# Starting an S5 and ConvFFN trunk on one core: the first modulation batches loaded ahead of x, low halves of x shared differently, column thirds dealt 4, 3, 3, 3, 3, 1, 0, and the first gating unit begun beside the last turns

## What is computed

```
mods = silu(c) @ w_ada + b_ada
h = x * (1 + scale) + shift
u = h @ s5_w_in                       # 64 groups of 16 channels
states = scan(a_bar, b_bar u)         # complex, 64 states a group
y = gelu(re(c_bar states) + d_skip u)
z = y @ w_glu
out = z[..., :1024] * sigmoid(z[..., 1024:])
x = layer_norm(ALPHA * x + gate * out)
```

## Time and profile before

| | |
|---|---|
| median of 3 runs | 2645.55 us (2645.07 to 2648.68) |
| profiled execution, its own time | 2644.4 us |
| its span in the profile | 2642.6 us |
| TensorE (PE) busy | 2444.6 us, 93% |
| VectorE (DVE) busy | 1441.1 us, 55% |
| GpSimd (POOL) busy | 1131.5 us, 43% |
| mean granted TensorE clock | 0.966 |

### The profile page before, as it was taken

How to read it: one execution, slowest core, us unless ns; L and a number is a source line. 1 busy time by engine, 2 the same in 40 slices (tenths; PEclk the granted TensorE clock), 3 DMA queues, 4 the chain that set the end, 5 groups by cost and what they waited for, 6 DMA issues and landing times.

```text
span 2642.6 us, 37011 instructions
## 1 busy us (share of the span) xinstructions
PE 2444.6 (93%) x15428; PEld 2334.2 (88%) x15428; DVE 1441.1 (55%) x1957; ACT 631.1 (24%) x1275; POOL 1131.5 (43%) x613
## 2 busy tenths in 40 slices
PE   3798899879999999999989999987999999999995
PEld 2688799679999999999968999976999999999993
DVE  6698321474555555555573344367455555555555
ACT  2433211242222222222121110103322222222213
POOL 4787343263443434343336333415544444444420
PEclk7899999989999999999989999988999999999998
DMA  5435533102222222221101221100111111111102
GB/s 215 152 117 139 185 105 110 51 25 72 80 80 74 79 79 73 80 72 57 64 17 53 75 78 48 41 26 15 57 48 48 45 44 48 49 48 45 44 25 72
DMA packets 90669, 187.28 MB, mean 71 GB/s; under 512 B 27664, under 2 KB 49936, under 8 KB 90384
## 3 DMA queue, kind: packets, MB, share of 16 engines
q1 hardware_dynamic: 80976, 175.23, 20.4%
q10 hardware_dynamic: 9536, 9.77, 1.1%
HBM read 170.66 MB, written 14.32 MB: 70 GB/s over the span
## 4 chain that ended last, share of the span: by engine, by line
PE 82%; DVE 8%; DVEq 2%; issue 2%; DMA 2%; ACT 1%; POOL 1%; SPq 1%; POOLq 1%; ACTq 0%
PE bank L669 17%; PE bank L671 17%; PE bank L670 17%; PE bank L912 8%; PE bank L913 7%; PE bank L914 7%; PE bank L931 2%; PE bank L633 1%; DVE X L1726 1%; DVE ROWS L1718 1%; DMA FST<-s_y 1%; DVE HL L1754 1%; DVE X L1712 1%; PE bank L639 1%; PE bank L976 1%
## 5 line engine op out<-in xcount | busy, mean ns | idle before, releaser
L669 PE MATMUL bank<-HH,WH 128*128 128x344 f32 x2880 | 924.5, 321 | 0.0
L670 PE MATMUL bank<-HL,WH 128*128 128x344 f32 x2880 | 919.9, 319 | 0.0
L671 PE MATMUL bank<-HH,WL 128*128 128x344 f32 x2880 | 919.8, 319 | 0.0
L493 POOL TENSOR_TENSOR WH<-RAW,ZERO 128x1024 fp32r<-128x1024 f32 x176 | 373.0, 2119 | 1191.2 <-DMA RAW<-in_wstream 1104.1
L1692 DVE SCALAR_TENSOR_TENSOR X<-bank,MOD,X 128x344 f32<-128x344 f32 (+1 forms) x624 | 355.5, 571 | 428.1 <-PE bank L914 295.6
L669 PEld LDWEIGHTS bank<-HH,WH 128*128 128x128 f32 x2880 | 540.9, 188 | 15.1 <-issue 13.4
L671 PEld LDWEIGHTS bank<-HH,WL 128*128 128x128 f32 x2880 | 541.3, 188 | 0.0
L670 PEld LDWEIGHTS bank<-HL,WH 128*128 128x128 f32 x2880 | 540.9, 188 | 0.0
L488 POOL TENSOR_TENSOR WL<-RAW,WH 128x1024 fp32r<-128x1024 f32 x188 | 504.4, 2683 | 49.0 <-ACT WH L1024 35.2
L912 PE MATMUL bank<-GH,WH 128*128 128x344 f32 x1248 | 409.5, 328 | 22.2 <-DVE X L1692 22.2
L913 PE MATMUL bank<-GL,WH 128*128 128x344 f32 x1248 | 402.4, 322 | 0.0
(11 more groups left out here) (286 smaller groups left out, 2420.9 us busy)
## 6 DMA issues: line engine op xcount, KB each, us to landing
RAW<-in_wstream SPq DMA_DIRECT2D x188, 512.0 KB, 3.6
ADA<-in_wada SPq DMA_DIRECT2D x20, 2048.0 KB, 9.6
FST<-in_wada SPq DMA_DIRECT2D x8, 1024.0 KB, 7.9
X<-in_xT SPq DMA_DIRECT2D x1, 4128.0 KB, 20.7
out_yT<-X SPq DMA_DIRECT2D x3, 1376.0 KB, 5.6
FST<-in_xT SPq DMA_DIRECT2D x8, 512.0 KB, 4.2
UT<-s_u SPq DMA_DIRECT2D x8, 512.0 KB, 6.0
s_y<-YG ACTq DMA_DIRECT2D x8, 512.0 KB, 2.9
```

What stands on the lines that cost most here:

```text
L493: ptt(WH[:, slot, :], RAW[:, slot, :], bc(ZERO[:, :], [128, 1024]), add).then_inc(s_hi, 1)
L669: pe.matmul(o, wh, hh, start=k == 0, stop=False)
L670: pe.matmul(o, wh, hl, start=False, stop=False)
L671: m = pe.matmul(o, wl, hh, start=False, stop=k == KC - 1)
```

## The change

On SP, all batches of w_ada move ahead of the chunks of x that they are not needed for, and b, H0 and x 6 and 7 change places. TensorE forms the products of batch 1 before the first unit. The sample columns of x are split by GpSimd alone. GpSimd keeps the low halves of x 0 and 1, VectorE takes 2 to 7 in between its small work; `sample_starts` moves behind `output_matrix(0)`. The table LO is built in two parts. The 17 thirds behind third 0 are dealt 4, 3, 3, 3, 3, 1, 0. Chunks 0 to 3 of gating unit 0 go into turn 6 and chunks 4 and 5 into turn 7, first for thirds 0 and 1 of the columns alone; the last third follows behind `toeplitz(7)`. In turn 6 GpSimd's `rotations(7)` stands behind `low_y(0)` and `low_y(1)`. The loads of y and of the toeplitz rows change places on SP, and the reload of x is cut into chunks 0 and 1 ahead of `load_y(7)` and the rest behind it. The diff, cut to what matters:

```diff
...
         BK = [ctx.enter_context(nc.psum_tensor(f"bank{i}", [128, 512], F32)) for i in range(8)]
         SMP_IN, SMP_OUT = BK[7][:, 256:320], BK[7][:, 320:352]
-        SMP_Y = BK[6][:, 0:NS * (KC - 2)], BK[7][:, 0:NS * 2]
...
             load_unit(0)
             load_unit(1)
+            load_first(1)
             load_x(0)
-            sp.dma_start(H0[:, :, :, :], h0T).then_inc(s_h0l, 16)
-            load_first(1)
             load_x(1)
             load_first(2)
-            for i in range(2):
-                sp.dma_start(BR[:, i], bT[i]).then_inc(s_cst4, 16)
             load_x(2)
             load_x(3)
             load_first(3)
+            for i in range(2):
+                sp.dma_start(BR[:, i], bT[i]).then_inc(s_cst4, 16)
             load_x(4)
             load_x(5)
+            load_x(6)
+            load_x(7)
             for dst, src in ((CR[:, 0], cS[0]), (CR[:, 1], cS[1]), (DSK[:, :], dT), (E16[:, :], eye16), (PM[:, :, :], pmask)):
                 sp.dma_start(dst, src).then_inc(s_cst2, 16)
-            load_x(6)
-            load_x(7)
+            sp.dma_start(H0[:, :, :, :], h0T).then_inc(s_h0l, 16)
             load_unit(2)
             load_unit(3)
...
-            load_u(2)
-            load_toeplitz(1)
-            for j in range(2, KC - 2):
+            for j in range(1, KC - 2):
+                load_u(j + 1)
                 load_toeplitz(j)
-                load_unit(j + 5)
-                load_u(j + 1)
+                load_unit(j + 6)
                 if j == 3:
                     load_ada4(1)
+            for k in range(3):
+                load_y(k)
+            load_u(KC - 1)
+            load_y(3)
+            load_y(4)
             load_toeplitz(KC - 2)
-            load_unit(KC + 3)
-            load_y(0)
-            load_y(1)
-            load_u(KC - 1)
-            load_y(2)
-            load_y(3)
+            load_ada4(2)
+            load_y(5)
             load_toeplitz(KC - 1)
-            load_y(4)
-            load_y(5)
-            load_ada4(2)
             load_y(6)
...
-            sp.dma_start(X[:, :, :], xT).then_inc(s_xl, 16)
+            sp.dma_start(X[:, 0:2, :], xT[:, 0:2, :]).then_inc(s_xl, 16)
             load_y(KC - 1)
+            sp.dma_start(X[:, 2:KC, :], xT[:, 2:KC, :]).then_inc(s_xl, 16)
...
-                ptt(HS[:, ks, :], HS[:, ks, :], MOD[:, ks, 1:9], add).then_inc(s_hsf, 1)
-            def low_sample_x(b):
-                ks = slice(2 * b, 2 * b + 2)
-                pool.wait_ge(s_hsh, b + 1)
+                ptt(HS[:, ks, :], HS[:, ks, :], MOD[:, ks, 1:9], add)
+                pool.drain()
+                pool.tensor_copy(HH[:, ks, SEQ:NT], HS[:, ks, :])
+                pool.drain()
                 ptt(HL[:, ks, SEQ:NT], HS[:, ks, :], HH[:, ks, SEQ:NT].bitcast(F32), sub).then_inc(s_hs, 1)
...
             low_half(1)
             sample_x(0)
             low_x(0)
-            low_sample_x(0)
             low_x(1)
+            sample_x(1)
             pool.wait_ge(s_pw, 1)
-            table(LO, 16)
-            sample_x(1)
-            low_x(2)
-            low_sample_x(1)
-            low_x(3)
+            table(LO, 1, 8)
+            sample_x(2)
+            table(LO, 8, 16)
+            sample_x(3)
+            low_half(2)
             pool.tensor_copy(HI[:, :, :, 1], LO[:, :, :, 16])
             pool.drain()
-            table(HI, 7)
-            for b in range(2, 4):
-                sample_x(b)
-                low_sample_x(b)
-            low_half(2)
+            table(HI, 1, 7)
             rotations(0)
             low_half(3)
             state_inputs(1)
-            for j in range(1, KC):
+            for j in range(1, KC - 1):
                 rotations(j)
                 low_half(j + 3)
-                if j < KC - 1:
-                    state_inputs(j + 1)
-            for k in range(KC - 1):
+                state_inputs(j + 1)
+            low_y(0)
+            low_y(1)
+            rotations(KC - 1)
+            for k in range(2, 6):
                 low_y(k)
+            low_half(KC + 2)
+            low_y(6)
             low_half(KC + 3)
...
-            def first_batch(b):
+            def first_products(b):
                 pe.wait_ge(s_first[b], 32)
+                if b:
+                    pe.wait_ge(s_fev, b)
                 for i in (0, 2, 4, 6, 1, 3, 5, 7):
...
                 m.then_inc(s_fprod, 1)
+            def first_sums(b):
                 pe.wait_ge(s_fev, b + 1)
...
-                if k < 4:
+                if k < 2:
                     pe.wait_ge(s_xsp, k + 1)
                 else:
-                    pe.wait_ge(s_xsd, k - 3)
+                    pe.wait_ge(s_xsd, k - 1)
...
             pe.wait_ge(s_scp, 1)
             pe.wait_ge(s_cst, 16 * N_CST)
-            first_batch(0)
+            first_products(0)
+            first_sums(0)
+            first_products(1)
+            first_sums(1)
             pe.wait_ge(s_unit, 2)
             first_units(0)
-            first_batch(1)
             first_units(1)
-            first_batch(2)
+            first_products(2)
+            first_sums(2)
             first_units(2)
-            first_batch(3)
+            first_products(3)
+            first_sums(3)
             for k in range(3, KC):
                 first_units(k)
...
-                if k == 0:
-                    pe.wait_ge(s_unit, N_GLU + u + 1)
-                    if u == 0:
+            def gate_chunk(u, k, thirds=(0, 1, 2)):
+                if k == 0 and u == 0:
+                    if 0 in thirds:
+                        pe.wait_ge(s_unit, N_GLU + 1)
                         pe.wait_ge(s_ev, 24)
+                    else:
                         pe.wait_ge(s_kr, KC)
-                    else:
-                        pe.wait_ge(s_g, KC)
-                        pe.wait_ge(s_yg, 2 * KC)
+                if k == 0 and u == 1:
+                    pe.wait_ge(s_unit, N_GLU + 2)
+                    pe.wait_ge(s_g, KC)
+                    pe.wait_ge(s_yg, 2 * KC)
                 if k < KC - 1:
                     pe.wait_ge(s_hl, k + 1)
                 else:
                     pe.wait_ge(s_hl7, 1)
-                pe.wait_ge(s_smp, 1 if k < KC - 2 else 2)
-                for t in range(3):
+                for t in thirds:
+                    if t == 2:
+                        pe.wait_ge(s_smp, 1 if k < KC - 2 else 2)
                     m = chunk(GATE[u][t][:, 0:TH], (N_GLU + u) % 4, k, t)
                     if k == KC - 1:
                         m.then_inc(s_up, 1)
...
             for j in range(KC - 1):
                 chunk_inputs(j)
                 impulse(j)
-                third(at)
+                if j < KC - 2:
+                    third(at)
+                else:
+                    gate_chunk(0, 0, (0, 1))
+                    gate_chunk(0, 1, (0, 1))
                 sample_inputs(j)
                 transpose_inputs(j + 1, 0)
-                if j < KC - 2:
+                if THIRDS[j] > 1:
                     third(at + 1)
-                else:
-                    toeplitz(j)
+                elif j == KC - 2:
+                    gate_chunk(0, 2, (0, 1))
                 transpose_inputs(j + 1, 1)
-                if j < KC - 2:
-                    toeplitz(j)
+                toeplitz(j)
                 if j in ADA_PE:
                     pe.wait_ge(s_wtev, 2 * j + 4)
                     ada_batch(ADA_PE[j], BK[6])
-                if 2 <= j < KC - 2:
-                    third(at + 2)
+                for i in range(2, THIRDS[j]):
+                    third(at + i)
+                if j == KC - 2:
+                    gate_chunk(0, 3, (0, 1))
                 if j in ADA_PE:
                     pe.wait_ge(s_apart, ADA_PE[j] + 1)
                     ada_batch_sum(BK[6], 0).then_inc(s_asum, 1)
                 sample_outputs(j)
                 outputs(j)
-                at += (2, 2, 3, 3, 3, 3, 1)[j]
+                at += THIRDS[j]
             j = KC - 1
-            pe.wait_ge(s_wtev, 2 * KC)
+            chunk_inputs(j)
+            impulse(j)
+            gate_chunk(0, 4, (0, 1))
+            pe.wait_ge(s_kr, KC)
             order_sample_y(0, KC - 2, 1)
-            chunk_inputs(j)
-            pe.wait_ge(s_smp, 1)
-            impulse(j)
-            for k in range(3):
-                gate_chunk(0, k)
             sample_inputs(j)
+            gate_chunk(0, 5, (0, 1))
             toeplitz(j)
-            for k in range(3, KC - 2):
-                gate_chunk(0, k)
+            for k in range(KC - 2):
+                gate_chunk(0, k, (2,))
             sample_outputs(j)
             outputs(j)
             for k in range(KC - 2):
...
+            def first_partial_sums(b):
+                act.wait_ge(s_fprod, b + 1)
+                if b:
+                    act.wait_ge(s_fsum, b)
+                act.activation(EVB[:, :], BK[6][:, :], ACT.Copy).then_inc(s_fev, 1)
...
-            first_mods(0)
             high_half(0)
```

(87 more changed lines are left out.)

8 lines of the change are left out of this document (removed).

## The result

The changed kernel takes 2614.98 us (median of 4 runs, 2612.1 to 2615.53) against 2646.07 of the kernel before in the same session (4 runs): a ratio of 0.9879, 95% interval [0.9862, 0.9896], so 31 us, or 1.2%, faster. The forecast was 2615 in a range of 2599 to 2634.

A forecast was written before the change was run, and what follows sets the result against it. Before 98.8 us the front was held by waits on GpSimd's tables, and the end by y 7's chain. Gains of 31 at `states(0)`, less 7.5, plus 1.5, plus 5.5 make 30.5 us: 2615 us, range 2599 to 2634.

The forecast's parts named there:

- What bounds the front: Front: TensorE's dependence on the tables goes; GpSimd's and VectorE's chains remain, and `states(0)` starts at 77, not 108.2.
- The terms of GpSimd's chain: Front: tables, rotations, one low half and sample columns add to 40.7 us from 31.3, plus 5 for VectorE's disturbance.
- which the change leaves where it was: Start of the front: the unit power, from which both chains run, stays at 31.3 us.
- The share of the port: Front: about 4 of 9.3 us of VectorE's work is added to GpSimd's when both run side by side.
- The shared port as a rival: Front: every VectorE instruction shuts GpSimd out, `states(0)` at 97, 20 us more lost, 2635 us; chance 0.13.
- Turn 0: First turn: TensorE gets two more thirds, 7.2 us; the turn becomes 30 us and the gain shrinks from 31 to 23.5.
- Turns 1 to 5: Middle turns: 1.5 us gained together, bounds 0 and 4, so `states(6)` starts 25 earlier, at 218.2.
- Turn 6: `states(7)` starts 28 us after `states(6)`, since TensorE waits for y's low halves behind gate chunks 2 and 3.
- The tail: From `outputs(7)` to chunk 7: 12.8 us for 19.3, y 7's store at 2.9, TensorE's own 11 just covered.
- If the store stays slow the whole is 6.5 less: Tail: if y 7's store is not shortened from 9.39 us, the total gain falls by 6.5 us.
- the rival of no change: Whole kernel: port shared whole and the reload still in the way of y 7's store, 2641.5 us; chance 0.05.
- slower rival: TensorE's clock drops after idle gaps and 80 us of its work in turns 1 to 4 slows, 2663 us; chance 0.04.

The follow-up runs named there:

- experiment 7: The changed kernel with VectorE's six low halves of x each made twice, one copy into a scratch tile: 2621.53 us.
- 8: The changed kernel with batch 1 of the first products back behind x 0, low halves left on VectorE: 2617.38 us.
- 9: The changed kernel with the low halves of x 2 and x 3 on GpSimd again: 2622.65 us.
- Experiment 2: The changed kernel with thirds dealt 2, 3, 3, 3, 3, 3, 0, so two in turn 0 and three in turn 5: 2623.24 us.
- Experiment 4: The changed kernel with gate chunks 2 and 3 behind impulse(7) instead of in turn 6: 2608.19 us.
- experiment 5: The changed kernel with x reloaded in one 4 MB transfer ahead of y 7, as before the change: 2616.07 us.

## Why the prediction was right

The time was met to 0.1 us, which is luck in part; the steps one by one:

- **What bounds the front: right.** The prediction said that TensorE's dependence on the tables goes away, and that GpSimd's chain alone then sets `states(0)`. Forecast 77, measured 79.36; the end of `rotations(0)` is the releaser. VectorE has 8.9 us of slack, so "the two chains have no slack of their own" holds for GpSimd's alone. TensorE's waits for sample columns are at most 1.2 us, under the 3 named.
- **The terms of GpSimd's chain: right in sum, wrong one by one.** Forecast and measured: three LO steps 12.5 and 10.3, the last 4.6 and 7.8, sample columns 2.6 and 5.9, low half 2.3 and 2.3, HI 9.2 and 12.4, rotations 9.5 and 7.2, and 5 for VectorE's work. The sum is 45.7, measured 45.8. The 9.5 for rotations and the 12.5 already held disturbance, and it fell on other steps now. The 2 us by which `states(0)` is late are the unit power: "which the change leaves where it was" fails, it came at 33.3 for 31.3 (the last section shows why).
- **The share of the port: too low.** I took 4 us lost for 9.3, 0.43; experiment 7 shows 0.74. It didn't show in the sum because two of the terms, LO's first steps and rotations, were too dear; that is luck. The shared port as a rival, 97 for `states(0)`, is out, though its mechanism is the right one (below).
- **What isn't in the sum by itself:** the prediction priced the front as a whole. Two parts of it have an experiment: the place of the first batch, 3.6 us (8), and the low halves of x 2 and 3, 7.8 us (9). How the other 17 or so of the 29 divide between the tables, the sample columns left to GpSimd, VectorE's order and the other loads, no run shows.
- **Turn 0: right.** `state_inputs(1)` is done at 89.02 (forecast 87), 9.8 behind `rotations(0)`; `states(1)` at 109.91 (107). Lost are 8.3 for 7.5. Experiment 2 shows the two thirds as the cause of most: without them `states(1)` is 6.3 earlier. From `state_inputs(1)` to the end of `chunk_inputs(1)` it is 20.7 for 19.7; behind its 12.0 us of idle time TensorE runs the first of these matmuls at the lower clock (0.65 as the mean of 79.36 to 98.80). The output matrix of turn 0 takes 10.9 us (90.35 to 101.3), as expected.
- **Turns 1 to 5:** 2.9 gained for 1.5, inside the bounds of 0 and 4; no turn got longer by more than 0.3.
- **Turn 6: right in kind and size.** 29.15 us for 28. The longest wait for y is 5.91 us for the 8 named, with 4.08, 1.54 and 0.17 beside it. Experiment 4 shows that it was avoidable, and worth 7 us at the end, not the 5 of turn 6 alone: turn 7 and the tail lost 3.99 and more to the same y.
- **The tail: near in size, wrong in cause.** The prediction took 12.8 us from `outputs(7)` to chunk 7, by y 7's chain with a store of 2.9, and held TensorE's own work in it, 11, to be "just covered". That step fails. Without y 7, TensorE needs 15.0:

```profile
264.79 2.06 PE L822 MATMUL bank<-GS,CA 64*128 64x128 f32 x32
268.23 0.40 PE L643 MATMUL bank<-HH,WH 128*128 128x344 f32 x1 [1.39 <-ACT YG L1173]
...
279.81 0.32 PE L643 MATMUL bank<-HH,WH 128*128 128x344 f32 x1
```

  The 72 matmuls from 268.23 to 279.81 are 11.6, but `outputs` itself and the 1.39 ahead of them come on top. The low half of y 7 is written at 279.12, 0.7 us before it is needed, with a store of 4.5. So TensorE's own work ends the tail. Of the 6.1 gained between `states(6)` and the batch behind the gate chunks, 0.4 comes ahead of `outputs(7)` (45.1 for 45.5), 4.3 between it and chunk 7 (15.0 for 19.3), and 1.4 on the last 18 matmuls (2.92 for 4.34 us): in the kernel before they stood behind the wait of 3.38 and ran at a mean clock of 0.66, now at 1.00. The prediction had no such term, and without it the gain is 4.7 for its 5.5; that 6.1 is so near is luck. "If the store stays slow the whole is 6.5 less", on which the rival of no change leant, was never put to the test, since the store didn't stay slow (experiment 5).
- **The clock: right.** The slower rival didn't come: the granted clock is

```profile
98.80:219.70 120.90, 112.90 (x1069) 0.97 0.48 143
219.70:248.85 29.15, 17.45 (x133) 0.71 0.52 162
```

  (PE busy, clock, DMA share, GB/s): a mean of 0.71 in turn 6, where TensorE stands idle for 12 of 29 us, and 0.97 from the middle of turn 0 to the end of turn 5. What a drop costs is seen in single rows, 3.37 us for a `toeplitz` of 2.05 in turn 7. It stayed in the turns where TensorE waits: 0.65 in the first 19.4 us of turn 0, 0.71 in turn 6, 0.77 in the first 15.2 us of turn 7.

## What to carry to other kernels

Follow a queue in both directions before you move work: late thirds didn't hurt the engine that they run on, they held the buffer that a load waits for, and with it every load queued behind. Where a small product of a slow engine (8 columns) is needed by a fast one, and comes back to it through a third engine, look at that circle first: TensorE waited 27.9 us for it before and 2.2 after, and two low halves of 2.4 us put back into it cost 7.8. And before two edits are summed, ask whether they cure the same idle time: the reload cut was worth 5 us alone and 1 at most beside the others.
